# Moving the cross attention's heads between its query tiles, and starting its output projection in four free PSUM banks

## What is computed

```python
def memory_cross_attention(h, mem_n, w_q, w_kv, w_o):
    q = (h @ w_q).reshape(B, T, XATTN_HEADS, XATTN_HEAD_DIM)
    k, v = jnp.split(mem_n @ w_kv, 2, axis=-1)
    ...
    s = jnp.einsum('bthd,bmhd->bhtm', q, k).astype(jnp.float32) * (XATTN_HEAD_DIM ** -0.5)
    p = jax.nn.softmax(s, axis=-1).astype(h.dtype)
    o = jnp.einsum('bhtm,bmhd->bthd', p, v).reshape(B, T, D_MODEL)
    return o @ w_o
```

## Time and profile before

| | us |
|---|---|
| median of 3 runs (2257.73 to 2259.71) | 2259.66 |
| the profiled execution's own time | 2259.86 |
| its span in the trace | 2257.7 |
| TensorE busy (matmuls) | 2097.1, 93% |
| DVE, ACT, POOL busy | 989.9, 921.7, 945.8 |
| mean granted TensorE clock | 0.969 |

### The profile page before, as it was taken

The page is one execution under the profiler, slowest core; times in us unless marked ns, Lnnn a source line. Parts: engine busy times, 40 slices in busy tenths (PEclk is TensorE's granted clock), DMA queues, the critical chain, the costliest instruction groups (busy, mean ns, idle before and its releaser), DMA issues.

```text
span 2257.7 us, 27865 instructions
## 1 busy us (share of the span) xinstructions
PE 2097.1 (93%) x9954; PEld 1719.7 (76%) x9954; DVE 989.9 (44%) x1101; ACT 921.7 (41%) x1094; POOL 945.8 (42%) x431
## 2 busy tenths in 40 slices
PE   3999989999999998999999999888889869999996
PEld 3788868787878777888888878787678557887885
DVE  7055532454544556211124377484661364343223
ACT  2366652223232342444422475563352325555421
POOL 3422224243434333444445376572374043444451
PEclk9999999999999999999999999898999979999998
DMA  7311112433333322323333222100333022232331
GB/s 266 94 57 57 57 56 86 153 107 132 116 133 130 111 83 76 93 93 102 93 103 102 87 73 72 50 1 1 119 105 122 10 65 66 93 96 91 111 102 46
DMA packets 56232, 203.69 MB, mean 90 GB/s; under 512 B 6240, under 2 KB 6368, under 8 KB 55904
## 3 DMA queue, kind: packets, MB, share of 16 engines
q1 hardware_dynamic: 56160, 202.70, 27.8%
HBM read 200.57 MB, written 2.10 MB: 90 GB/s over the span
## 4 chain that ended last, share of the span: by engine, by line
PE 81%; DVE 9%; ACT 5%; issue 2%; POOL 2%; DMA 1%; DVEq 0%; ACTq 0%; SPq 0%; POOLq 0%
PE acc L1719 21%; PE acc L1721 20%; PE acc L1720 20%; PE aux L1719 2%; PE aux L1721 2%; PE aux L1720 2%; ACT sp L529 2%; PE acc L1928 2%; PE aux L1776 2%; PE aux L2152 1%; DVE cfy L1375 1%; PE aux L1783 1%; POOL sqacc L455 1%; PE aux L1842 1%; PE acc L2311 1%
## 5 line engine op out<-in xcount | busy, mean ns | idle before, releaser
L468 POOL TENSOR_TENSOR w_lo<-raw,w_hi 128x1024 fp32r<-128x1024 f32 x324 | 796.1, 2460 | 1192.4 <-ACT w_hi L529 1190.9
L1719 PE MATMUL acc<-x_hi,w_hi 128*128 128x512 f32 x1544 | 618.2, 400 | 12.7 <-DVEq L994 3.8
L1720 PE MATMUL acc<-x_lo,w_hi 128*128 128x512 f32 x1544 | 607.3, 393 | 0.0
L1721 PE MATMUL acc<-x_hi,w_lo 128*128 128x512 f32 x1544 | 606.6, 393 | 0.0
L529 ACT ACTIVATE w_hi<-raw 128x1024 fp32r<-128x1024 f32 x324 | 342.7, 1060 | 555.3 <-PE acc L1721 441.1
L1719 PEld LDWEIGHTS acc<-x_hi,w_hi 128*128 128x128 f32 x1544 | 294.1, 190 | 87.7 <-issue 9.1
L1721 PEld LDWEIGHTS acc<-x_hi,w_lo 128*128 128x128 f32 x1544 | 293.5, 190 | 63.1
L1720 PEld LDWEIGHTS acc<-x_lo,w_hi 128*128 128x128 f32 x1544 | 294.0, 190 | 58.8
L529 ACT ACT_TABLE_LOAD x86 | 110.3, 1283 | 54.5 <-DVE tn L1678 20.8
L1678 DVE SCALAR_TENSOR_TENSOR tn<-acc,cols,tn 128x511 f32<-128x511 f32 x88 | 65.9, 749 | 122.1 <-ACT tn L529 115.7
L1025 DVE SCALAR_TENSOR_TENSOR adac<-ada,c_act,adac 128x1024 f32<-128x1024 f32 x42 | 65.7, 1564 | 97.4 <-DMA ada<-in_ada 96.5
(11 more groups left out here) (376 smaller groups left out, 3228.1 us busy)
## 6 DMA issues: line engine op xcount, KB each, us to landing
raw<-in_weights SPq DMA_DIRECT2D x324, 512.0 KB, 3.5
ada<-in_ada SPq DMA_DIRECT2D x48, 512.0 KB, 3.6
resid<-in_x SPq DMA_DIRECT2D x1, 2048.0 KB, 11.7
out<-resid SPq DMA_DIRECT2D x8, 256.0 KB, 2.0
decay<-in_tables SPq DMA_DIRECT2D x4, 256.0 KB, 3.6
memf<-in_mem SPq DMA_DIRECT2D x1, 1024.0 KB, 4.9
angles<-in_tables SPq DMA_DIRECT2D x1, 512.0 KB, 3.5
small<-in_small SPq DMA_DIRECT2D x1, 320.0 KB, 3.8
```

Source lines behind the costliest of these rows:

```text
L468: nc.gpsimd.tensor_tensor(w_lo[s][:], raw[s][:], w_hi[s][:].bitcast(F32), ALU.subtract).then_inc(lo_ready, 1)
L1719: M(out, a_hi, b_hi, start=first, stop=False)
L1720: M(out, a_hi, b_lo, start=False, stop=False)
L1721: return M(out, a_lo, b_hi, start=False, stop=last)
```

## The change

PE now makes queries 0 to 2, the scores of head 0, queries 3 and 4, the scores of head 1, turns head 0, and so on: `attend` is split into `turn_probabilities` and `value`, and the five last query tiles, and later quarters and halves of projection tiles, stand between the parts of the heads. `project(n, first, end)` accumulates the feature tiles `first` to `end` of output tile `n` straight into bank `n` of `aux`, for n from 0 to 3; the tiles 4 to 7 use `acc` as before. `Q_AT` and `V_AT` number the turns of the two `acc` banks. DVE's and ACT's lists are rewritten to the same order; DVE copies the first four output tiles from `aux`. SP's and POOL's lists are the same as before.

```diff
--- before.py
+++ after.py
@@ -145,11 +145,14 @@
 ]
 
 TILES = [
-    ("first", 188), ("gdn_in", 25), ("mix_out", 8), ("kv", 8), ("xq", 8), ("x_val", 8), ("xo", 8),
+    ("first", 188), ("gdn_in", 25), ("mix_out", 8), ("kv", 8), ("xq", 8), ("x_val", 8), ("xo", 4),
     ("up", 44), ("down", 8),
 ]
 
 AB, CFM, KVQ, GATE = 0, 1, 9, 21
+
+
+Q_AT, V_AT = (0, 1, 2, 3, 4, 5, 8, 9), (6, 7, 10, 11, 12, 13, 14, 15)
 LEVELS = 7
 COLS = [
     ("c", 8), ("b_ada", 48), ("g_norm1", 8), ("b_branch", 16), ("g_norm2", 8), ("g_final", 8),
@@ -923,10 +926,6 @@
                 for b in range(2):
                     bk = 2 * half + b
                     own["vm_ready"].own(f(vm[:, b, half * T:(half + 1) * T], aux[:, bk * T:(bk + 1) * T]))
-            for n in range(KT):
-                split_hi(At(U0["xq"] + n + AHEAD))
-
-
             XSC = (KT // XH * P) ** -0.5
 
             def exps(h):
@@ -936,18 +935,36 @@
                             scale=XSC, bias=xcols[:, h % 2, 0, t:t + 1], accum_out=xcols[:, h % 2, 1, t:t + 1])
                     (step if t < NB - 1 else own["px_ready"]).own(ins)
 
-            own["tile_done"].skip(6)
-            exps(0)
-            for h in range(XH):
+            def turned(h):
                 own["px_turned"].next()
                 own["pxt_ready"].own(f(pxt[:, h % 2, :], aux[:, 4 * T:6 * T]))
-                if h + 1 < XH:
-                    exps(h + 1)
+
+            def values_hi(h):
                 for d in range(2):
-                    t = At(T0["x_val"] + 2 * h + d)
                     own["tile_done"].next()
-                    own["xo_hi_ready"].own(f(xo_hi[:, 2 * h + d, :], bank(t)))
-            for n in range(8):
+                    own["xo_hi_ready"].own(f(xo_hi[:, 2 * h + d, :], bank(At(T0["xq"] + V_AT[2 * h + d]))))
+
+            own["tile_done"].skip(6)
+            for n in range(4):
+                split_hi(At(U0["xq"] + n + AHEAD))
+            exps(0)
+            split_hi(At(U0["xq"] + 4 + AHEAD))
+            split_hi(At(U0["xq"] + 5 + AHEAD))
+            exps(1)
+            turned(0)
+            split_hi(At(U0["xq"] + 6 + AHEAD))
+            values_hi(0)
+            split_hi(At(U0["xq"] + 7 + AHEAD))
+            exps(2)
+            turned(1)
+            split_hi(At(U0["xo"] + AHEAD))
+            values_hi(1)
+            turned(2)
+            exps(3)
+            values_hi(2)
+            turned(3)
+            values_hi(3)
+            for n in range(1, 8):
                 split_hi(At(U0["xo"] + n + AHEAD))
             root(1.0 / D)
             residual_squares()
@@ -1592,6 +1609,9 @@
 
                 step.own(V.tensor_copy(dst, bank(t)))
                 free(t)
+                sublayer_sums(dst)
+
+            def sublayer_sums(dst):
                 step.own(V.tensor_tensor(sqt[:], dst, dst, ALU.mult))
                 step.own(V.tensor_tensor(sqacc[:], sqacc[:], sqt[:], ALU.add))
 
@@ -1619,9 +1639,9 @@
             end_squares()
             invert()
             next_residual(yv, norm_g[1], norm_g[2])
-            for n in range(KT):
+            def queries(n):
                 dve.wait_ge(unit_used, U0["xq"] + n + 1)
-                evict(qx[:, n, :], At(T0["xq"] + n), own["qx_ready"])
+                evict(qx[:, n, :], At(T0["xq"] + Q_AT[n]), own["qx_ready"])
 
 
             def row_max(h):
@@ -1641,25 +1661,39 @@
 
             def out_low(h):
                 for d in range(2):
-                    t, k = At(T0["x_val"] + 2 * h + d), 2 * h + d
+                    t, k = At(T0["xq"] + V_AT[2 * h + d]), 2 * h + d
                     own["xo_hi_ready"].next()
                     own["xo_ready"].own(V.tensor_tensor(xo_lo[:, k, :], bank(t), xo_hi[:, k, :].bitcast(F32), ALU.subtract))
                     free(t)
 
             own["tile_done"].skip(KT)
+            for n in range(3):
+                queries(n)
             row_max(0)
+            normalize(0)
+            queries(3)
+            queries(4)
             row_max(1)
-            normalize(0)
-            for h in range(XH):
-                if h + 1 < XH:
-                    normalize(h + 1)
-                if h + 2 < XH:
-                    row_max(h + 2)
-                out_low(h)
+            normalize(1)
+            queries(5)
+            out_low(0)
+            queries(6)
+            row_max(2)
+            normalize(2)
+            queries(7)
+            out_low(1)
+            row_max(3)
+            normalize(3)
+            out_low(2)
+            out_low(3)
             step.own(V.memset(sqacc[:], 0.0))
             for n in range(KT):
                 dve.wait_ge(unit_used, U0["xo"] + n + 1)
-                sublayer_tile(At(T0["xo"] + n), yv_o[:, n, :])
+                if n < 4:
+                    step.own(V.tensor_copy(yv_o[:, n, :], aux[:, n * T:(n + 1) * T]))
+                    sublayer_sums(yv_o[:, n, :])
+                else:
+                    sublayer_tile(At(T0["xo"] + n - 4), yv_o[:, n, :])
             end_squares()
             invert()
             normed_residual(yv_o, norm_g[3], norm_g[4])
@@ -2277,14 +2311,12 @@
             token_tiles(At(U0["kv"] + 12), (2, 3), mem_hi, mem_lo)
             spread_rs()
             own["x_ready"].next(KT)
-            tiles("xq", KT, T0["xq"], x_hi, x_lo)
-
-
-            own["km_ready"].next(KT)
-            own["vm_ready"].next(4)
-            own["qx_ready"].next(KT)
+
+            def queries(n):
+                tile(At(U0["xq"] + n), At(T0["xq"] + Q_AT[n]), x_hi, x_lo)
 
             def scores(h):
+                own["qx_ready"].next(2)
                 if h >= 2:
                     own["px_ready"].next()
                 b = (h % 2) * 2 * T
@@ -2294,7 +2326,7 @@
                               kmt[:, 2 * h + k, :], start=k == 0, stop=k == 1)
                 m.then_inc(S["xs_done"], 1)
 
-            def attend(h):
+            def turn_probabilities(h):
                 own["pxn_ready"].next()
                 if h:
                     pe.wait_ge(S["pxt_ready"], h)
@@ -2303,23 +2335,62 @@
                         m = nc.tensor.transpose(aux[:, (4 + mt_) * T + t * P:(4 + mt_) * T + (t + 1) * P],
                                                 px[:, h % 2, t, mt_ * P:(mt_ + 1) * P], ident)
                 m.then_inc(S["px_turned"], 1)
+
+            def value(h):
                 own["pxt_ready"].next()
                 for d in range(2):
-                    t, k = At(T0["x_val"] + 2 * h + d), 2 * h + d
+                    t, k = At(T0["xq"] + V_AT[2 * h + d]), 2 * h + d
                     wait_bank(t)
                     for mt_ in range(2):
                         m = M(bank(t), vm[:, mt_, k * P:(k + 1) * P], pxt[:, h % 2, mt_ * T:(mt_ + 1) * T],
                               start=mt_ == 0, stop=mt_ == 1)
                     m.then_inc(S["tile_done"], 1)
 
+            def project(n, first, end):
+
+                wh, wl = weights(At(U0["xo"] + n))
+                for k in range(first, end):
+                    m = three(aux[:, n * T:(n + 1) * T], wt(wh, k), wt(wl, k), xo_hi[:, k, :], xo_lo[:, k, :],
+                              k == 0, k == KT - 1)
+                if end == KT:
+                    m.then_inc(unit_used, 1)
+
+            for n in range(3):
+                queries(n)
+            own["km_ready"].next(KT)
+            own["vm_ready"].next(4)
             scores(0)
+            queries(3)
+            queries(4)
             scores(1)
-            for h in range(XH):
-                attend(h)
-                if h + 2 < XH:
-                    scores(h + 2)
-            lead("xo", T0["xo"], xo_hi, xo_lo, own["xo_ready"])
-            tiles("xo", KT, T0["xo"], xo_hi, xo_lo, first=4)
+            turn_probabilities(0)
+            queries(5)
+            value(0)
+            queries(6)
+            scores(2)
+            turn_probabilities(1)
+            queries(7)
+            value(1)
+            scores(3)
+            turn_probabilities(2)
+            own["xo_ready"].next(4)
+            project(0, 0, 4)
+            project(1, 0, 4)
+            value(2)
+            turn_probabilities(3)
+            project(2, 0, 4)
+            project(3, 0, 4)
+            value(3)
+            own["xo_ready"].next(2)
+            project(0, 4, 6)
+            project(1, 4, 6)
+            own["xo_ready"].next(2)
+            project(0, 6, 8)
+            project(1, 6, 8)
+            project(2, 4, 8)
+            project(3, 4, 8)
+            for n in range(4, KT):
+                tile(At(U0["xo"] + n), At(T0["xo"] + n - 4), xo_hi, xo_lo)
             stat_spread()
             stat_spread()
             lead("up", T0["up"], x_hi, x_lo, own["x_ready"])
```

## The result

| | before | changed |
|---|---|---|
| median, us | 2258.69 (4 runs, 2257.33 to 2259.71) | 2241.83 (4 runs, 2239.09 to 2245.23) |
| profiled execution / its span | 2259.86 / 2257.7 | 2241.88 / 2240.1 |
| first query to last projection matmul (the stage) | 134.43 | 119.11 |
| last projection to first feed-forward matmul (the tail) | 30.09 | 28.88 |

The ratio is 0.9925, with an interval of 0.9909 to 0.9941. The direction held, and so did the mechanism in the stage; the range did not.

A forecast was written before the change was run, and what follows sets the result against it. PE was taken as the bound, idle or slowed in the heads. -15.1 - 0.23 + 0.2 + 0.45 = -14.7, with 0.1 kept for signals -14.6; 2259.86 - 14.6 = 2245.3 us, range 2243.0 to 2250.0.

The forecast's parts named there:

- What bounds the kernel: PE carries 81% of the chain of waits; the stage's one hole is the heads, busy 35.37 of 46.4 us.
- The heads' waits: Softmax chains in the heads hidden under query and projection work on PE: 15.1 us saved, including the slow clock.
- The allowances of 0.2 for banks and 0.1 for signals: Time added back to the sum: 0.2 us where values to queries are tight for banks, 0.1 for small signals.
- The lost 15.1 us go: In the heads, 46.4 us less 31.3 of work; all saved, the clock's part included, as no gap is left.
- 31.3 us of head work: PE's work in four heads, each 3.45 us of scores, 3.50 of values and 0.87 of turn.
- The first pair's bank: The projection's first pair of tiles waited 0.23 us for its bank; with four banks this goes.
- DVE behind POOL's splits: In the projection, DVE alternates with four POOL splits and comes late, costing PE 0.45 us at tile 6.
- the end of the last tile to the column sum stays 2.88: Behind the projection: DVE is level again at tile 6, so this stretch keeps its 2.88 us.
- handovers kept no wait: Rival: PE still waits before values 0 to 3, 4 x 1.4 = 5.6 us, giving 2250.9; chance 0.10.
- DVE did not become the bound: Rival: in the projection seven splits each cost DVE 2.4 us in full, 3.6 us more, 2248.9; chance 0.10.
- no gap moved into a tile: Rival: softmax gaps and slow clock move into full-rate tiles, 7.9 us a head, 2276.9 us; chance 0.04.
- the time would come back elsewhere: Rival: the 15.1 us return elsewhere, for instance as later feed-forward tiles; classed as no change, chance 0.03.

The follow-up runs named there:

- the heads alone: Changed kernel with heads still between query tiles, but the projection put back behind all heads, in the two acc banks; 2248.68 us, ratio 0.9949.
- the projection alone: Changed kernel with all eight queries first, heads in the old order, and the projection's early pieces kept; 2250.87 us, ratio 0.9978.
- the squares run: Changed kernel with squares of projection tiles 0 to 3 made from the PSUM bank and yv_o; 2237.26 us, once more 2240.01 us.
- the clock filled in head 0: Kernel before with 16 matmuls that nobody reads added where PE waited in head 0; 2256.04 us, ratio 0.9992.
- the added eight: Changed kernel with squares from PSUM, plus eight matmuls that nobody reads ahead of projection tile 4; 2244.82 us, ratio 0.9952.
- ACT late: Changed kernel with the pxt copy on ACT done four times in place of once in every head; 2245.88 us, ratio 0.9946.
- six banks: Changed kernel with projection tiles 4 and 5 in banks 4 and 5 of aux; 2240.6 us, ratio 0.9924.

## Why the prediction was right or wrong

**What bounds the kernel:** right. PE's idle time and slow clock in the heads were nearly the whole loss of the stage, and they are gone.

**The heads' waits:** right in place, 0.8 us too small in size. The stage gave 15.32; with tile 6's 0.53 added (what its removal gave) and the first pair's 0.23 taken off, the heads gave 15.6, for which the sum had 15.1 less 0.3 of allowances, 14.8. The allowances of 0.2 for banks and 0.1 for signals were hardly needed. "The lost 15.1 us go" rested on 31.3 us of head work, from rows taken inside the heads. Between other tiles it is shorter from start to start: scores 1720.29 - 1717.03 = 3.26 where 3.45 stood, a turn 0.79 for 0.87, values 3.35 for 3.50, in all four heads 30.0 us for the 31.3. About half of that comes back in the tiles around, which the prediction kept at their old length: the queries take 44.2 where they took 43.8 without their wait, the projection without its waits 44.3 for 44.1. So some 0.6 us of the 0.8 are a net gain of the new order, and the rest the allowances. The runs bore out the layout's other figures in part: 10.2 us for the heads alone, 1.2 us of margin on ACT and 2.8 us for the clock, but not the 4.6 us of the projection alone, which held 2.0 that were not its own. One figure of the prediction is off: the stage before was 134.43 us and not 134.7, so "about 120" should have read 119.8.

**The first pair's bank:** gone, as said (0.23).

**DVE behind POOL's splits:** right. 0.45 was forecast for tile 6, PE began it 0.43 later than it could, and both ways of removing the wait shortened the stage by 0.5. The Trainium skill's rule ("SBUF — State Buffer", "SBUF: two separate sides") was weighed as a rival, and the trace and the squares run agree with it as the page words it: two SBUF inputs wait, one input in PSUM does not. The prediction set the copy's 0.69 against the page; its source is PSUM, so it fits the rule too.

**The step that failed** is "the end of the last tile to the column sum stays 2.88", taken as if all behind it stayed as well. 2.88 did stay (2.89). What follows it did not: 0.43 us came from the first column sums (1.48 to 1.05) and 0.44 from the spread (2.08 to 1.64), by the clock that was still at 1.00. Some 0.35 came from the idle time ahead of DVE's first low part, which goes with the early projection's code at any clock, and whose cause stays open. The sum lacked a term of 1.2 us, and the bounds had none for the clock outside the stage.

**The range's lower end** was 2243, built on the forecast and the lowest of three runs. By its own terms it was 2257.73 - 14.9 = 2242.8, rounded up. With the tail's 1.2 it would have been 2241.6, just under the result. The forecast itself, with the 16.6 us that stage and tail gave, would have been 2259.86 - 16.6 = 2243.3, still 1.4 over the median of four. 1.2 of that is the base: the prediction started from the profiled execution, 2259.86, and the median of the kernel before came out at 2258.69. The rest is scatter, of a size that three runs (2 us between them) did not show, and 23 did (10.6 us).

**The rivals:** handovers kept no wait; DVE did not become the bound; no gap moved into a tile, and the clock stayed at 1.00 even where waits of 1.8 us were put in. That the time would come back elsewhere fell too: more came than the stage gave.

## What to carry to other kernels

Where one engine bounds a kernel and idles for a chain of small steps on others, lay its list out from start to start with the neighbours' independent work between the steps, and compare each step's due time with the chain. Laid out from the profiles at hand, this gave the stages of seven variants within 0.5 us, though in one it missed a wait of 2.30 us and was saved by other gains, so look at the rows and not at the total alone. Add the stretch behind the change to the sum, since moving its start moves where the clock falls in it, and take step lengths from the surroundings in which they will stand. Where a DVE operation with two SBUF inputs waits beside GpSimd's, let one input come from PSUM (0.69 us for 2.06 here), or give its consumers more banks.

## What the runs showed of the hardware

- The tail goes mostly with the clock over its first 5 us. That clock was 0.78 with the clock filled in head 0 (tail 30.48), 0.83 and 0.84 in the kernel before (30.09, 29.99), 0.84 with the heads only (29.99), 0.83 with the added eight (29.71), 0.93 with ACT late (29.32), 0.97 with the projection only (29.10), and 1.00 in the changed kernel (28.88, 28.72), with six banks (28.41) and with squares from PSUM (28.38, 28.37). Each of the three kernels that were profiled twice repeats its value, and eight unread matmuls ahead change it. So the place at which the clock fell here was the same for the same code, and a kernel's gain can carry a microsecond that the edited work did not give. The 0.3 to 0.4 us between 29.71 and the others at 0.83 and 0.84 are DVE's idle time of 0.40, which is not the clock's.
- Single waits of 1.17 to 2.30 us of PE between dense stretches left the clock at 1.00. Waits of 3.07 and 1.17 close together brought it to 0.55 over the next 7.3 us in the kernel before, and to 0.77 with the projection only: the same waits do not cost the same in two kernels.
- Copies from PSUM, and squares with one PSUM input, took 0.69 us beside POOL's splits; squares and sums with two SBUF inputs that met a split took 1.33 to 2.79.
- Code that is the same in all versions ended between 1697.66 and 1704.10 us, a scatter larger than most of the effects measured here. Between the two profiles of the changed kernel it is 3.5 us, and DVE's instructions, compared one by one, show that it arises in two places: 1.3 us between 236 and 387 us of the span, 2.1 between 840 and 933.
